# A triangular inverse by doubling whose products take only the columns of each second block

## The reference, cut to what matters

```python
def wkv7(r, w, k, v, a, b):
    # S_t = S_{t-1} diag(w_t) + (S_{t-1} a_t) b_t^T + v_t k_t^T ;  y_t = S_t r_t
    def step(S, inp):
        sa = jnp.einsum('bhvk,bhk->bhv', S, a_t)
        S = S * w_t[:, :, None, :] + sa[..., None] * b_t[:, :, None, :] + v_t[..., None] * k_t[:, :, None, :]
        y = jnp.einsum('bhvk,bhk->bhv', S, r_t)
        return S, y
```

## Time and profile before

| what | us |
| --- | --- |
| median of 3 runs | 2038.81 |
| lowest and highest | 2034.72, 2039.42 |
| the profiled execution, its own time | 2039.6 |
| its span in the profile | 2037.8 |

### The profile page before, as it was taken

How to read it: one execution, slowest core, us unless ns; L and a number is a source line. 1 busy time by engine, 2 the same in 40 slices (tenths; PEclk the granted TensorE clock), 3 DMA queues, 4 the chain that set the end, 5 groups by cost and what they waited for, 6 DMA issues and landing times.

```text
span 2037.8 us, 35141 instructions
## 1 busy us (share of the span) xinstructions
PE 1972.1 (97%) x14308; PEld 1602.2 (79%) x14308; DVE 1164.2 (57%) x1797; ACT 784.0 (38%) x1399; POOL 213.0 (10%) x166
## 2 busy tenths in 40 slices
PE   6999999989999999998999999999999999999997
PEld 2777899977787877775777887877888878888885
DVE  6689766566534354467575747485464266556423
ACT  5777333334322122337632222234343234444211
POOL 3000222200202021003302012020000010000001
PEclk9999999999999999998999999999999989999998
DMA  5321000222333322230144544544531122332421
GB/s 193 118 92 42 2 4 4 81 89 84 104 94 94 102 93 83 91 99 24 65 175 152 174 148 150 183 151 131 178 114 32 62 91 86 103 102 83 146 92 42
DMA packets 61004, 201.48 MB, mean 99 GB/s; under 512 B 8000, under 2 KB 11200, under 8 KB 59584
## 3 DMA queue, kind: packets, MB, share of 16 engines
q1 hardware_dynamic: 60096, 192.93, 28.6%
q10 hardware_dynamic: 768, 6.55, 1.0%
HBM read 190.68 MB, written 6.42 MB: 97 GB/s over the span
## 4 chain that ended last, share of the span: by engine, by line
PE 71%; issue 17%; DVE 8%; POOL 2%; ACT 1%; DMA 0%; DVEq 0%; POOLq 0%; SPq 0%; ACTq 0%
PE bank L2022 17%; PE bank L2024 17%; PE bank L2023 17%; POOL HS L2831 2%; PE bank L2238 2%; PE bank L2206 1%; PE bank L2253 1%; DVE xl L1280 1%; PE bank L2210 1%; DVE wlo L1250 1%; DVE HR L1610 1%; PE bank L2507 1%; PE bank L2017 1%; DVE GBZ L1427 1%; PE bank L2527 1%
## 5 line engine op out<-in xcount | busy, mean ns | idle before, releaser
L1250 DVE TENSOR_TENSOR wlo<-raw,whi 128x1024 fp32r<-128x1024 f32 x270 | 327.7, 1223 | 572.8 <-ACT whi L696 571.6
L696 ACT ACTIVATE whi<-raw 128x1024 fp32r<-128x1024 f32 x270 | 282.3, 1057 | 709.3 <-PE bank L2024 696.5
L2022 PE MATMUL bank<-inh,whi 128*128 128x512 f32 x1200 | 471.0, 392 | 1.8 <-DVE inl L1487 1.6
L2024 PE MATMUL bank<-inh,wlo 128*128 128x512 f32 x1200 | 467.2, 389 | 0.0
L2023 PE MATMUL bank<-inl,whi 128*128 128x512 f32 x1200 | 467.2, 389 | 0.0
L2022 PEld LDWEIGHTS bank<-inh,whi 128*128 128x128 f32 x1200 | 225.3, 188 | 58.2 <-issue 6.6
L2024 PEld LDWEIGHTS bank<-inh,wlo 128*128 128x128 f32 x1200 | 225.3, 188 | 47.3
L2023 PEld LDWEIGHTS bank<-inl,whi 128*128 128x128 f32 x1200 | 225.3, 188 | 46.7 <-issue 0.7
L2022 PE MATMUL bank<-hidh,whi 128*128 128x512 f32 x576 | 228.6, 397 | 8.2 <-DVE HR L1610 5.5
L2024 PE MATMUL bank<-hidh,wlo 128*128 128x512 f32 x576 | 224.6, 390 | 0.0
L2023 PE MATMUL bank<-hidl,whi 128*128 128x512 f32 x576 | 224.3, 389 | 0.0
(11 more groups left out here) (423 smaller groups left out, 2871.9 us busy)
## 6 DMA issues: line engine op xcount, KB each, us to landing
raw<-in_mlp_w SPq DMA_DIRECT2D x128, 512.0 KB, 3.6
ADW<-in_w_ada SPq DMA_DIRECT2D x32, 768.0 KB, 5.0
raw<-in_w_up SPq DMA_DIRECT2D x44, 512.0 KB, 3.6
raw<-in_w_in SPq DMA_DIRECT2D x28, 512.0 KB, 3.6
raw<-in_a_w_rkv SPq DMA_DIRECT2D x24, 512.0 KB, 3.5
raw<-in_w_down SPq DMA_DIRECT2D x22, 512.0 KB, 3.6
raw<-in_a_wo SPq DMA_DIRECT2D x8, 512.0 KB, 7.6
raw<-in_b_wq SPq DMA_DIRECT2D x8, 512.0 KB, 3.4
```

What stands on the lines that cost most here:

```text
L696: act.activation(whi[u % SLOTS][:, :], raw[u % SLOTS][:, :], ACT.Copy).then_inc(w_hi, 1)
L1250: dve.tensor_tensor(lo[:, :], r[:, :], h[:, :].bitcast(F32), ALU.subtract).then_inc(w_lo, 1)
L2022: pe.matmul(o, w[:, wc], xh, start=start, stop=False)
L2024: return pe.matmul(o, r[:, wc], xh, start=False, stop=stop)
```

## The change

The products of a level take only the second block of each pair: 32 of the 64 columns. Four small helpers form the views. `later(ap, lv)` takes, of each `4 << lv` columns, the second half; `part(ap, lv)` cuts 32 contiguous columns into the same pieces, so that both sides of a matmul have one shape. In the banks and in QS the 32 columns lie contiguously; in Z they are read and written in 32 / (2 << lv) runs of 2 << lv elements: 16 runs of 2 at level 0, 8 of 4, 4 of 8, 2 of 16, and one of 32 at level 4, for each of the 8 pairs.

Rows and stationary columns stay at 64 at all levels, and the masks, the transposes and the order of the work stay as they were: PE, DVE, ACT and POOL issue the same number of instructions in the same order.

```diff
+        def later(ap, lv):
+            return ap.rearrange("p (a two b) -> p a two b", two=2, b=2 << lv)[:, :, 1, :]
+        def later_all(ap, lv):
+            return ap.rearrange("p c (a two b) -> p c a two b", two=2, b=2 << lv)[:, :, :, 1, :]
+        def part(ap, lv):
+            return ap.rearrange("p (a b) -> p a b", b=2 << lv)
+        def part_all(ap, lv):
+            return ap.rearrange("p (c a b) -> p c a b", c=CB, b=2 << lv)
...
-                        act.activation(QS[x][:], pairs(PB[x][:]), ACT.Copy).then_inc(ai.sem, ai.step(("q", g, lv, x)))
+                        act.activation(QS[x][:, :, 0:HC // 2], pairs(PB[x][:, 0:CB * HC // 2]), ACT.Copy).then_inc(ai.sem, ai.step(("q", g, lv, x)))
...
-                        dve.tensor_tensor(z, z, pairs(PB[2 + x][:]), ALU.add).then_inc(di.sem, di.step(("z", g, lv, x)))
+                        zl = later_all(z, lv)
+                        dve.tensor_tensor(zl, zl, part_all(PB[2 + x][:, 0:CB * HC // 2], lv), ALU.add).then_inc(di.sem, di.step(("z", g, lv, x)))
...
+            def narrow(cb):
+                return slice(cb * HC // 2, (cb + 1) * HC // 2)
...
-                                mm = pe.matmul(PB[x][hs, tok(cb)], LM[x][lv % 2][hs, cb, :], GBZ[j % 4][hs, cb, HC:P], start=True, stop=True)
+                                mm = pe.matmul(part(PB[x][hs, narrow(cb)], lv), LM[x][lv % 2][hs, cb, :], later(GBZ[j % 4][hs, cb, HC:P], lv), start=True, stop=True)
...
-                                mm = pe.matmul(PB[2 + x][hs, tok(cb)], TI[x][hs, cb, :], QS[x][hs, cb, :], start=True, stop=True)
+                                mm = pe.matmul(PB[2 + x][hs, narrow(cb)], TI[x][hs, cb, :], QS[x][hs, cb, 0:HC // 2], start=True, stop=True)
```

## The result

The changed kernel takes 2044.01 us (median of 15 runs, 2040.73 to 2046.96), the kernel before in the same session 2038.66 us (15 runs, 2034.72 to 2040.80). The ratio is 1.0028, 95% interval 1.0021 to 1.0034: 0.28% slower, where I had forecast 0.35% faster. The time lies outside the range of 2024 to 2038 us.

The account below looks back on a forecast made before the run. Each level was taken as bound by a loop through PE and DVE, 4.27 us, falling to 3.76 with PE the bound. Gains 6.1 - 0.3 + 1.3 = 7.1 us gave 2031.7 us, 0.35% less; range 2024 to 2038 us.

Parts of the forecast that it names:

- The bound and the pace: Inverse levels: a loop through PE and DVE takes 4.27 us; weight loads keep 32 records at 0.93 us, PE slack 0.54.
- The add: DVE in each level: 256 elements take 0.42 us against up to 0.70, saving 0.54 us for two adds, short runs free.
- rival (c): DVE's adds: short runs cost 8 cycles each, a level takes 4.73 us, whole time 2045 us; chance 0.05.
- Groups 0 to 2: Levels of the first three groups: 6.1 us gained, less 0.3 for a PE stall in group 1.
- Rival (a): PE's products: records come 25.3 ns apart, 0.81 us a group of 32, whole time 2024.6 us; chance 0.14.
- rival (d): PE in the levels: halved activity lowers the clock to 1.2 GHz, up to +65 us, 2104 us; chance 0.07.
- no gain there: Group 3 after levels 0 and 1: PE already late from early sums and stalls; the rest of group 3 gains 1.3 us.
- rival (b): Levels: PE has no slack left; stalls, waits or short runs take 1 to 3 us each, 2034.5 us; chance 0.14.
- The range: Whole kernel time: 2024 to 2038 us.

Follow-up runs that it names:

- e10: Changed kernel with only 16 columns moving in both products, the add replaced by a maximum of Z with itself; 2087.16 us in one run.
- e11: Changed kernel with 32 stationary columns in both products, the add replaced by a maximum of Z with itself; 2038.30 us in one run.
- e2: Kernel before with products, copy and add narrowed to 32 columns in group 3 only; 2049.90 us, ratio 1.0042 to the kernel before.
- e6: Kernel before with only the G2 and weight loads waiting for the last product of group 3's levels; 2042.59 us, ratio 1.0008.
- e8: Changed kernel with 64 columns in products and copy of group 3's levels 2 to 4, the add still half; 2036.06 us, ratio 0.9978 to before.
- e5: Kernel before with only DVE's add halved, and the G2 and weight loads waiting for group 3's last level product; 2035.47 us, ratio 0.9975.
- e4: Changed kernel with the G2 and weight loads waiting for the last product of group 3's levels; 2036.02 us, ratio 0.9978 to the kernel before.
- e3: Kernel before with only DVE's add halved, products and copy keeping 64 columns; 2035.88 us, ratio 0.9972.
- e9: Changed kernel with 64 columns in products and copy of group 3's levels 0 to 2, the add still half; 2035.12 us, ratio 0.9981 to before.
- e1: Changed kernel with group 3 back at all 64 columns in products, copy and add; 2037.05 us, ratio 0.9980 to the kernel before.
- e7: Changed kernel with 64 columns in products and copy of group 3's levels 0 and 1, the add still half; 2040.71 us, ratio 0.9992 to before.

## Why the prediction was wrong

- **The bound and the pace: right.** A level was a loop through DVE, PE had 0.54 us of slack, and its groups stay at 0.93 us for 32 records. e10 and e11 show that the stationary side sets the pace, as rows 6 and 7 had suggested; that it is the load itself stays argued.
- **The add: right.** 0.42 us against 0.70 at the most, in all five levels; no run length costs anything, so rival (c) is out.
- **Groups 0 to 2: right within the noise.** 5.2 us instead of 5.8 in the one pair. In one execution the start of group 3 moves by some us: e2, whose groups 0 to 2 are those of before, has it at 399.20, before 396.35, and e6, the same there too, 394.59. From the first product of group 0 to the first of group 3 these three take 154.6 to 157.6 us, the eight traces with the short add 149.5 to 153.3: 4 us less in the mean.
- **Rival (a): out here.** Nothing ran closer than 28.6 ns with 64 stationary columns. The Trainium skill, TensorE: Matmul & The Clock Gate, section "Wait — 56ns, not 53.3ns?", says that starts are never closer than about 25 ns however few columns move. This trace disagrees: e11's lie 18.3 ns apart, with 64 rows and 32 stationary columns, alternating between two row groups. (In the sum of this rival the 0.95 and 1.15 us of the earlier trace rows carry each other's names; their sum is as it should be.) The measurement decides.
- **The step that failed: rival (d), the granted clock, at 0.07.** The mechanism and the break-even were there ("14 us at 1.2 GHz eat the whole gain"; it was 30.7), and so was the danger of it in the wrong place: I asked whether halved activity would make the clock fall in a level, and answered with a stretch in which PE was busy 1.57 of 4 us at 1.00. In groups 0 to 2 the clock did hold. But the row tells of a clock that had not yet fallen. I didn't ask what a stretch must do to bring it back. That group 3 meets stalls of 1.78 and 1.23 us was on the table; I booked them as "no gain there", and not as the places where the clock is at stake. The price of a group of records at 1.2 GHz was 1.71 us, not 1.87, which changes nothing in the argument. With group 3 at +9.2 instead of -1.3 us, the sum is 5.2 - 9.2 = -4.0, about the 4.2 us late that the trace shows behind the scan.
- **The range.** Its upper end rested on rival (b). A case whose price reached +65 us had been left out entirely, for 0.07 of chance.

What stays open: the exact condition of the fall. At 32 columns it came after 1.82 us of stall in the kernel after and after 0.54 us in e2, and not after 0.54 us in the kernel after and e8. At 64 columns it didn't come after 1.78, 1.50 and 2.04 us in the levels, but after 1.96 us in the recurrence of e5 and e6, where e4 passed 1.96 and 2.59 us. I can say that a pause precedes it at 32 columns, none over 0.07 us is needed at 16, and that which pause does it can't be told from these traces. No run separates the stall from the transfers that run with it in group 3. The tail behind the scan (from the first `HS` to the end) also varies between 1497 and 1503 us from kernel to kernel, without a change in its code: the three at 1502.7 (after, e3, e6) had a clock of 0.72 from 1640 to 1670 us, but e9, at 1502.9, had 0.76, so the dip explains it in part at most. So of the 5.4 us between the medians 4.2 are explained; for the rest I have only this one execution.

None of the variants that beat the kernel before, e3 (0.9972), e5 (0.9975), e4 and e8 (0.9978), e1 (0.9980) and e9 (0.9981), can be told from the others. e3 is the simplest: it takes the gain where it is, on DVE, and leaves TensorE's stream as it was.

## What to carry to other kernels

Where the pace of TensorE doesn't follow the moving columns (here 28.6 to 29.2 ns a record from 64 down to 16), fewer of them save no time and leave the array emptier: narrow the instructions of the engine that closes the loop (here DVE's add), not the products. Before making a dense TensorE stretch thinner, look for every pause before and inside it, and price the whole stretch at half the clock from the first pause on, not only the pause. A row in which the clock is held tells nothing on whether the same stream would bring it back. And where a profile names a releaser, ask the program whether the engine waits for it at all: e7's mask was made during the pause, not waited for.

## What the runs showed of the hardware that was not expected

- A stream without gaps and 32 of 64 columns wide keeps the 2.4 GHz in the levels of groups 0 to 2 (some 19 us each), but once at 1.2 GHz it stays there for as long as it lasts: 30.7 us, 37.4 us in e2, 23.8 us in e7. With 64 columns behind it the clock is back after 6.7 us in e8. With 16 columns it isn't even kept (e10).
- Float32 records with 64 rows and 32 stationary columns start 18.3 ns apart; with 64 and 64 it is 28.6 to 29.2 ns, whether 16, 32 or 64 columns move.
- While or just after large transfers run, TensorE stands still for 1.0 to 2.6 us at a time without any wait that the profile shows, and these stalls follow the transfers when they are moved (e4 to e6). Stalls of up to 0.5 us come without transfers too (0.27 us in e4, 0.45 in e6), and longer ones in e11's denser stream (0.74 to 1.63 us in group 0).
